# Moving two chunk divisions of each expert from the unit before it into its first unit, in a mixture-of-experts stage

## The reference

```python
    gu = lax.ragged_dot(xs, w_gu, group_sizes) + b_gu[e_sorted]
    g, u = gu[:, :EXPERT_FF], gu[:, EXPERT_FF:]
    g = jnp.minimum(g, SWIGLU_LIMIT)
    u = jnp.clip(u, -SWIGLU_LIMIT, SWIGLU_LIMIT)
    act = (u + 1) * (g * jax.nn.sigmoid(SWIGLU_ALPHA * g))
    out = lax.ragged_dot(act, w_down, group_sizes) + b_down[e_sorted]
    out = out * gate_w.reshape(-1)[order][:, None].astype(out.dtype)
    y = jax.ops.segment_sum(out, src, num_segments=n_tok)
```

## Time and profile before

| | |
|---|---|
| median of 3 runs | 2624.65 us (2620.83 to 2624.91) |
| profiled execution | 2624.58 us, of which the span of the core's instructions is 2622.9 |
| TensorE | 91% of the span busy, mean granted clock 0.966 |
| VectorE | 59% |
| ScalarE | 51% |
| GpSimd | 32% |
| expert stage | from about 941 us to 2567 us |

### The profile page before, as it was taken

One profiled execution on the slowest core, in us unless ns is written; L12 is line 12 of the kernel. 1 busy time (PEld: TensorE's weight loads), 2 busy tenths in 40 slices (PEclk: granted clock), 3 DMA queues, 4 the chain that ended last, 5 costly groups with the idle time before them and its releaser, 6 DMA issues.

```text
span 2622.9 us, 55795 instructions
## 1 busy us (share of the span) xinstructions
PE 2398.5 (91%) x19131; PEld 1349.1 (51%) x19132; DVE 1548.6 (59%) x1837; ACT 1337.6 (51%) x1396; POOL 833.8 (32%) x946
## 2 busy tenths in 40 slices
PE   6999987799989969999998989899888999999991
PEld 3555554577755535554454545454444555555550
DVE  2222237566636675516437191857787777899975
ACT  1111144356632255416446181856787767888861
POOL 1222222500003353323333243334334443434322
PEclk9999989999999969999999999999999999999995
DMA  8000043420032286617547292969898888999974
GB/s 325 19 18 18 9 149 130 136 80 0 0 119 93 91 292 218 233 31 245 195 160 280 59 360 69 362 221 359 323 363 320 324 330 315 334 393 397 389 278 176
DMA packets 180296, 538.49 MB, mean 205 GB/s; under 512 B 20720, under 2 KB 37538, under 8 KB 180190
## 3 DMA queue, kind: packets, MB, share of 16 engines
q1 hardware_dynamic: 150668, 487.80, 49.2%
q0 software_dynamic: 26656, 46.85, 8.1%
q10 hardware_dynamic: 2916, 3.14, 0.3%
HBM read 493.12 MB, written 45.20 MB: 205 GB/s over the span
## 4 chain that ended last, share of the span: by engine, by line
PE 56%; DVE 7%; issue 4%; ACT 2%; DMA 1%; ACTq 0%; POOL 0%; DVEq 0%; POOLq 0%
PE psum L2121 45%; PE psum L2005 5%; DVE arena L1863 5%; PE psum L2110 2%; PE psum L2105 2%; PE psum L2099 1%; ACT arena L1667 1%; PE psum L2026 0%; DVE arena L1967 0%; DVE arena L1968 0%; PE psum L2014 0%; DVE arena L1981 0%; DVE arena L1930 0%; DMA arena<-expert_inputs,arena 0%; DVE arena L1920 0%
## 5 line engine op out<-in xcount | busy, mean ns | idle before, releaser
L2121 PE MATMUL psum<-arena 128*64 128x512 bf16 x12528 | 1421.0, 382 | 72.5 <-DVE arena L1863 37.0
L2121 PEld LDWEIGHTS psum<-arena 128*64 128x64 bf16 x12528 | 717.9, 111 | 727.1 <-DVE arena L1863 66.1
L1863 DVE TENSOR_TENSOR arena<-arena 128x2048 bf16<-128x2048 f32 x384 | 863.1, 2287 | 197.3 <-ACT arena L1667 197.2
L1667 ACT ACTIVATE arena<-arena 128x2048 bf16<-128x2048 f32 x384 | 722.6, 1904 | 104.5 <-DVE arena L1863 68.5
L1576 POOL DMA_INDIRECT expert_sums<-arena x90 | 186.1, 2068 | 635.9 <-issue 611.5
L560 PE MATMUL psum<-arena 128*128 128x512 f32 (+2 forms) x864 | 300.5, 506 | 1.1 <-ACT arena L416 1.1
L560 PEld LDWEIGHTS psum<-arena 128*128 128x128 f32 x864 | 151.7, 192 | 134.5 <-issue 129.8
L1920 DVE TENSOR_TENSOR arena<-psum,arena 128x512 bf16<-128x512 f32 x87 | 59.8, 688 | 228.1 <-ACT arena L1714 228.1
L1546 POOL DMA_INDIRECT arena<-expert_inputs,arena x88 | 108.4, 1231 | 193.5 <-PE psum L2099 173.0
L1725 ACT ACTIVATE arena<-psum,arena 128x512 f32<-128x512 f32 x87 | 59.2, 681 | 204.7 <-PE psum L2121 204.7
L1710 ACT ACTIVATE arena<-psum 128x1024 bf16<-128x1024 bf16 x87 | 88.3, 1015 | 139.6 <-issue 139.6
(11 more groups left out here) (289 smaller groups left out, 2169.6 us busy)
## 6 DMA issues: line engine op xcount, KB each, us to landing
arena<-in_w_gu SPq DMA_DIRECT2D x256, 1024.0 KB, 15.7
arena<-in_w_down SPq DMA_DIRECT2D x128, 1024.0 KB, 11.8
arena<-in_w_ada SPq DMA_DIRECT2D x12, 2048.0 KB, 9.8
arena<-in_x_sample SPq DMA_DIRECT2D x16, 512.0 KB, 3.4
arena<-in_w_in SPq DMA_DIRECT2D x3, 2048.0 KB, 20.3
expert_sums<-arena SPq DMA_DIRECT2D x10, 512.0 KB, 6.6
expert_inputs<-arena SPq DMA_DIRECT2D x10, 512.0 KB, 2.8
x_after_mixing<-arena SPq DMA_DIRECT2D x9, 512.0 KB, 2.6
```

Of the source, the lines that this page charges most:

```text
L1667: nc.scalar.activation(high(e, p, c), raw[p][c], ACT.Copy).then_inc(sem(f"hi_made{c}"), 1)
L1863: nc.vector.tensor_tensor(w_lo[p][c], raw[p][c], high(e, p, c), ALU.subtract).then_inc(sem(f"lo_made{c}"), 1)
L2121: last = nc.tensor.matmul(bank(b)[group(g)], parts[part][:, cols], w[:, kk, g * H:(g + 1) * H], start=False, stop=(k == KT - 1 and part == 1))
```

## The change

An expert's first unit now divides its own chunks 8, 9, 10, 11 and chunks 0, 1, 2 of the next expert (seven in all, before: 10, 11 and 0 to 3, six). Its last unit divides chunks 3 to 7 of the next expert (five, before: 4 to 9, six). The prologue of the stage divides chunks 0 to 7 of expert 0 instead of 0 to 9. The places of the divisions between the other steps of ScalarE and VectorE change with it. On ScalarE the request for the gate and up bias rows, with its wait for `used4`, goes behind the copies that follow the sigmoid.

```diff
@@ chunks_to_divide
             if first:
-                yield e, p, 10
-                yield e, p, 11
+                for c in range(8, CHUNKS):
+                    yield e, p, c
                 if not final(e):
-                    for c in range(4):
+                    for c in range(3):
                         yield e + 1, 1 - p, c
             if last:
-                for c in range(4, 10):
+                for c in range(3, 8):
                     yield e + 1, 1 - p, c
@@ ScalarE, ahead of the first unit
-                for c in range(6, 10):
+                for c in range(6, 8):
                     hi(0, 0, c)
@@ ScalarE, body
                     if last:
-                        divide(2 if first else 1)
+                        divide(3 if first else 1)
                     if not opening(j):
                         act_hi(j - 1)
                     sigmoid(j)
+                    divide(3 if first and last else 2)
                     if last:
                         wait(act, sem("used4"), n)
                         bias_gu(following)
-                    divide(2)
                     if opening(j):
...
                         keep_x(j + 1)
-                    divide(2 if first else 1)
+                    divide(2)
                     if not opening(j):
                         result(j - 1)
@@ VectorE, ahead of the first unit
-                for c in range(3, 10):
+                for c in range(3, 8):
                     lo(0, 0, c)
@@ VectorE, body
                     if last:
-                        divide(1)
+                        divide(3 if first else 1)
                     if not opening(j):
                         act_lo(j - 1)
                     if last:
```

## The result

| | before | after |
|---|---|---|
| median of 7 runs each | 2624.65 us (2620.23 to 2628.78) | 2636.65 us (2631.09 to 2639.32) |
| ratio, 95% interval | | 1.0041 (1.003 to 1.0052) |
| profiled execution | 2624.58 us | 2631.09 us |
| expert stage, first gate bias (L2110) to the last down bias (L2110) | 1619.08 us | 1631.44 us |
| the eight single-unit places together | 649.73 us | 655.71 us |

The change makes the kernel 12.0 us slower by the medians (8 to 14 us by the interval). The sign and the range were right (2627 to 2664 forecast). The size was not: 21.9 us forecast, 12.0 measured. The profiled execution of after is the fastest of its seven. Its stretch ahead of the first unit, by whose end nothing edited has run, was 5.9 us shorter than in the profile of before (941.40 and 935.53 us; over all profiles of this study it lies between 934.7 and 945.5).

The account below looks back on a forecast made before the run. VectorE's remainder chain was taken to bound the places around single-unit experts, TensorE the long stretch at the end. Single-unit places +10.3, two-unit experts +11.3 and start +0.3 made +21.9 us on 2624.58: 2646.5 us, range 2627 to 2664.

Parts of the forecast that it names:

- 3.30 us wait in N: TensorE's wait before the single unit's down product, run in the next expert's first unit; forecast to disappear.
- It can't begin before the result copy's wait is over: ScalarE's 3.95 us register walk into a single unit starts only after the previous unit's result copy; first copy at 1521.05.
- The seventh remainder: Two-unit experts: seven VectorE remainders instead of six before L1920, +2.2 us against a margin of 1.48 us.
- the two-unit term: Eleven two-unit experts, each +1.03 us because L1920 comes later in the second unit: +11.3 us in sum.
- gate waiting for bias rows: TensorE's gate product held up by late bias rows; listed among the signs that the forecast is wrong.
- ScalarE's result copy and sequencer waits put 0.4 us more into the row of copies: Single-unit places: 0.4 us added before L1920 in the next expert's second unit, which was forecast at 1574.5.
- about +0.25 for the copies that follow the result copy: Two-unit experts: 0.25 us added to the seventh remainder's 2.2 us, putting L1920 at 2415.35.
- The start: Units 0 and 1: two divisions leave the prologue, one more remainder ahead of L1920; +0.3 us, bounds 0 and 2.2.
- ScalarE gets back its wait in L, which is worth nothing, as TensorE sets the pace there: Later bias request frees ScalarE in the unit before a single-unit expert; claimed gain nothing.
- The walk hidden: Rival: the queue does the register walk during the result copy's wait; 2620 us (13%, no change) or 2609 us (7%, faster).
- The clock: Rival, 14%: new 2.4 us waits before down products slow TensorE's clock, 1.69 us at eight places, 13.5 us: 2660 us.
- rival 2: The clock rival: slow TensorE clock after the new waits before down products, 13.5 us more, 2660 us, 14%.

Follow-up runs that it names:

- run 6: Kernel after, with the two register loads for the bias requests moved from the body's head to behind sigmoid and `keep_x`: 2620.06 us against before's 2626.24, ratio 0.9975.
- run 4: Kernel after, with L1920 ahead of chunk 3's remainder in last units of larger experts and the bias request directly behind sigmoid: 2631.24 us, ratio 1.002 to before.
- run 2: Kernel after, with the bias request back directly behind sigmoid, so the new division alone: 2632.64 us against before's 2625.35, ratio 1.0034.
- Run 7: Kernel before, with only expert 0's chunks 8 and 9 moved from the prologue into its first unit: one run, 2628.18 us.
- run 1: Kernel before, with only the bias request moved behind the two division copies that follow sigmoid: 2615.89 us against 2625.35, ratio 0.9962.
- run 3: Kernel after, with L1920 ahead of chunk 3's remainder in the last unit of larger experts: 2634.9 us against before's 2625.35, ratio 1.0033.
- run 5: Kernel after, with chunk 11's copy ahead of the activation copy in single units: 2631.09 us against before's 2625.35, ratio 1.0026.
- run 9: Kernel after, with request directly behind sigmoid, L1920 ahead of chunk 3's remainder, chunk 11's copy early, register loads late: 2605.08 us, ratio 0.992 to before.
- run 10: Kernel before, with only the two register loads for the bias requests moved later: 2609.79 us against 2625.13, ratio 0.9938.
- run 8: Kernel before, old division, with late bias request, late register loads and chunk 8's copy ahead of the last unit's result copy: 2594.16 us, ratio 0.9876.

## Why the prediction was right in sign and wrong in size

The replay of the place was close. Times of after at expert 7, shifted by 3.67 us onto the clock of before:

| step | forecast | measured |
|---|---|---|
| first remainder of S (chunk 8) | 1523.1 | 1522.93 |
| L1920 for L's down product | 1529.7 | 1529.54 |
| wait ahead of it | 2.4 | 2.17 |
| VectorE's idle ahead of chunk 11 | 1.3 | 1.17 |
| end of chunk 7's remainder in N | 1553.6 | 1553.25 |
| 3.30 us wait in N | gone | gone |
| L1920 in M | 1574.5 | 1573.65 |
| wait in M, ahead of N's down product | 2.4 | 2.03 |
| M ends | 1580.4 | 1579.59 |

**What was right.** "It can't begin before the result copy's wait is over": the walk is exposed by 3.95 us, and run 6 shows that shortening it moves every place. The first copy of S came 5.24 us behind the result copy (5.3 forecast). The seventh remainder is the two-unit term: run 4 took it out of the chain and the term was gone. The bias rows are late in N at all places and hidden (run 2): "gate waiting for bias rows", named there as a sign of being wrong, was seen and meant nothing for the time.

**The step that failed** is a term of the sum, in two places: "ScalarE's result copy and sequencer waits put 0.4 us more into the row of copies", and "about +0.25 for the copies that follow the result copy". There is no such cost on VectorE's chain: both terms measured 0. The rows of before already had it from remainder to remainder: six took 13.33 us and seven take 15.54, 2.2 for one more and nothing else. At the two-unit experts this was 11 x 0.25 = 2.8 of the 2.9 us that the term was over (11.3 forecast, 8.4 measured). At the places it was 8 x 0.4 = 3.2. There N's L1920 also came 1.17 us earlier than before (1553.18), not 0.75, and 1572.62 - 1.17 + 2.2 is the measured 1573.65 with no room for the 0.4. That is another 8 x 0.4, so with M's end 0.81 us below the forecast 6.5 in all. Two falls of the clock in M, at experts 3 and 5 (83.27 and 83.21 us against 81.5), gave back 2 x 1.69 = 3.4. The remaining 1.2 of the 4.3 (10.3 - 6.0) is the place at expert 5 of before, which with 82.44 us was that much longer than its like (81.28) and was carried over into the forecast; the prediction, which gives 80.55 or 81.28 for a place, didn't look at it.

**The start** was put at +0.3, as if unit 0 kept its length. It is -2.0 (units 0 and 1), 2.3 off. Two remainders less in the prologue let GpSimd's small copies through sooner (below), and unit 1's gather with them: in after it is issued 14.9 us behind the start of unit 0, before 19.6 us. Run 7 shows the 3 us in unit 0; what they are worth at the end of unit 1 depends on the divisions behind `keep_x`. The size isn't firm: over the profiles units 0 and 1 take 46.6 to 48.1 us with the old start and 43.6 to 46.5 with the new one.

4.3 + 2.9 + 2.3 = 9.5 us, the whole gap between 21.9 and the stage's 12.4.

**"ScalarE gets back its wait in L, which is worth nothing, as TensorE sets the pace there"** was wrong as reasoning, though it cost the sum nothing. Alone the move is worth 9.5 us (run 1): an engine that doesn't set the pace in L still decides how early S begins. The prediction read that the walk of before began at 1517.8 and took the two copies for its cover, but didn't ask what held it until then: the last copy's wait for chunk 7's remainder. With the new division it is worth nothing for another reason, the walk that waits for the result copy (run 2). The 12 us of the change are the new division without help from the move.

**The rivals.** The walk hidden: refuted. The clock: it cost time at two places of eight. There M's down product, behind a wait of 2.0 us, was 1.69 us slower; at the other six the same wait had no fall behind it. But the clock fell somewhere in all eight places of after, and these other falls are hidden behind VectorE's chain: L's down product took 7.06 us at experts 5 and 9, as the prediction had it for L, and N's gate product 6.5 to 8.0 us at the other six, behind a wait of 3.7 to 4.2 us for bias rows. At expert 7, with a granted clock of 0.82:

```profile
1536.29 6.50 PE L2121 MATMUL psum<-arena 128*64 128x512 bf16 x48
```

Over the profiles of the new division it fell in M at two places (after and runs 2, 3 and 5, not always at the same experts) or at none (runs 4, 6 and 9), and only in run 9, where the waits are 1.1 and 1.6 us, nowhere in the eight places. In before it fell at six, in run 1 at five, but run 1 has a wait of 3.31 us at expert 7 without a fall. What picks the place stays open. The Trainium skill (TensorE: Matmul & The Clock Gate, HAM oscillation) describes a kernel in which blocks of products alternate with waits that are longer than the blocks, and in which the slow clock comes back at every wait. The waits of rival 2 are shorter than the blocks (2.0 to 2.2 us beside 5.37), so 2660 us did not follow from that case, and the trace shows the fall behind them at two places of eight.

## What to carry to other kernels

An instruction that waits for another engine, standing last ahead of a walk to the next body, exposes the whole walk (3.95 us here): leave something behind it whose data is there, and put a register load beside the request that needs it (run 10: -15.3 us by the medians, of which its profile shows 8.5 at the places). Work in a stage that another engine paces is not free to delay if it decides how early the next stage can begin. Before adding a term to a chain, look whether the row that gave the step's length already holds it.

## What the runs showed of the hardware that was not expected

**GpSimd's small copies wait for VectorE's remainders.** GpSimd ahead of unit 1's gather, before and after. VectorE ran four remainders from 947.53 to 956.43 in before; in after two of them ended at 946.49.

```profile
952.01 2.27 POOL L1570 COPY arena<-arena 128x6 f32<-128x6 f32 x1
...
961.01 1.22 POOL L1546 DMA_INDIRECT arena<-expert_inputs,arena  x1 [0.98 <-POOL arena L1598]
```

```profile
946.48 0.19 POOL L1570 COPY arena<-arena 128x6 f32<-128x6 f32 x1
...
950.41 3.04 POOL L1546 DMA_INDIRECT arena<-expert_inputs,arena  x1 [0.98 <-POOL arena L1598]
```

The same copy of 128 x 6 takes 2.27 us beside a remainder, about the length of one (2.29), and 0.19 us once VectorE has ended its own. The Trainium skill (SBUF — State Buffer, Who interferes with whom) says that a VectorE instruction with two inputs in SBUF, as the subtraction is, contends with a GpSimd instruction that reads SBUF, and that the lock on the ports they share is exclusive; the trace agrees (2.27 against 0.19 us).

**A request for 12 KB of bias rows** takes 4.3 to 4.8 us from its issue to its first use at the two-unit experts of run 3, where TensorE waits for it, and 3.7 to 5.9 us at the places of after. That is more than the 2.6 us of a 512 KB store and less than the 6.4 us of the gather.

**The walk begins when the last wait ahead of it is over.** ScalarE's queue does register work while copies ahead of it still run, but it passes none whose wait is open, at expert 7 in all six traces read for it (before, after, runs 1, 6, 8 and 10). In before it began at 1517.8, when chunk 7's remainder, for which the last copy ahead waits, had ended at 1517.74; in run 1, where that remainder was done before, at 1516.6; in after right with the start of the result copy (1512.07):

```profile
L1391 ACTq ALU_OP  x2: 35/35/35, 1512.1 to 1514.3; - x2
```

Of the walk's 3.95 us behind the result copy 1.41 were two register loads (run 6), and with one division copy in between the rest was done while that copy ran (run 8, "issue" 0.25 us).
